# FFN gate and up computed by token for chunks 0 to 9, with the product turned by VectorE and sixteen SBUF transfers

## What is computed

```python
def swiglu(x, w_gate, w_up, w_down):
    return (jax.nn.silu(x @ w_gate) * (x @ w_up)) @ w_down
...
        y = swiglu(rms_norm(h, g[0]), ffn_w_gate[i, 0], ffn_w_up[i, 0], ffn_w_down[i, 0])
        h = h + 0.5 * rms_norm(y, g[1])
```

## Time and profile before

| | |
|---|---|
| median of 3 runs | 1010.06 us (1009.65 to 1010.57) |
| the profiled execution | 1009.73 us |
| its span, first to last instruction | 1007.9 us |
| TensorE busy | 998.5 us, 99% |
| VectorE, ScalarE, GpSimd busy | 638.5, 519.8, 116.7 us |
| granted TensorE clock | 1.000 |
| DMA, mean | 188 GB/s, 189.55 MB |

### The profile page before, as it was taken

One profiled execution on the slowest core, in us unless ns is written; L12 is line 12 of the kernel. 1 busy time (PEld: TensorE's weight loads), 2 busy tenths in 40 slices (PEclk: granted clock), 3 DMA queues, 4 the chain that ended last, 5 costly groups with the idle time before them and its releaser, 6 DMA issues. The chain is left out here.

```text
span 1007.9 us, 13834 instructions
## 1 busy us (share of the span) xinstructions
PE 998.5 (99%) x5701; PEld 850.5 (84%) x5701; DVE 638.5 (63%) x768; ACT 519.8 (52%) x709; POOL 116.7 (12%) x214
## 2 busy tenths in 40 slices
PE   8999999999999999999999999999999999999997
PEld 7888888898777888888889888888888789888886
DVE  5666565757796765556576555557568776565654
ACT  5544445644674564444464544445457555444452
POOL 1000000222373200000030000001103320000000
PEclk9999999999999999999999999999999999999999
DMA  9767778367404465557735555592485346565551
GB/s 272 250 204 250 235 254 295 114 188 221 157 2 126 134 216 194 193 183 239 264 100 191 187 190 194 182 331 87 146 280 165 136 132 195 181 207 173 204 178 73
DMA packets 138422, 189.55 MB, mean 188 GB/s; under 512 B 7442, under 2 KB 120439, under 8 KB 138360
## 3 DMA queue, kind: packets, MB, share of 16 engines
q1 hardware_dynamic: 133734, 172.83, 52.3%
q0 software_dynamic: 4480, 15.77, 4.7%
q10 hardware_dynamic: 146, 0.07, 0.0%
HBM read 185.99 MB, written 1.09 MB: 186 GB/s over the span
## 5 line engine op out<-in xcount | busy, mean ns | idle before, releaser
L815 DVE TENSOR_TENSOR wlo<-raw,whi 128x2048 fp32r<-128x2048 f32 x140 | 321.2, 2294 | 121.2 <-ACT whi L554 121.2
L1239 PE MATMUL ps<-xhl,whi 128*128 128x512 f32 (+1 forms) x1664 | 370.5, 374 | 0.0
L1239 PEld LDWEIGHTS ps<-xhl,whi 128*128 128x128 f32 x1664 | 293.1, 188 | 55.2 <-issue 2.4
L554 ACT ACTIVATE whi<-raw 128x2048 fp32r<-128x2048 f32 x145 | 276.9, 1910 | 28.9 <-DMA raw<-in_fox_w_in 9.0
L1239 PEld LDWEIGHTS ps<-xhl,wlo 128*128 128x128 f32 x1536 | 196.1, 191 | 6.9 <-issue 0.4
L1239 PE MATMUL ps<-xhl,wlo 128*128 128x256 f32 x1536 | 199.8, 283 | 0.0
L1239 PE MATMUL ps<-whi,hhi 128*128 128x512 f32 x320 | 124.9, 390 | 0.0
L1239 PE MATMUL ps<-wlo,hhi 128*128 128x512 f32 x320 | 124.9, 390 | 0.0
L1239 PE MATMUL ps<-whi,hlo 128*128 128x512 f32 x320 | 124.5, 389 | 0.0
L1239 PE MATMUL ps<-whi,xhl 128*128 128x512 f32 (+1 forms) x464 | 114.1, 373 | 0.3 <-ACT xhl L594 0.3
L1239 PEld LDWEIGHTS ps<-whi,xhl 128*128 128x128 f32 x464 | 81.1, 190 | 15.8 <-issue 1.9
(11 more groups left out here) (176 smaller groups left out, 803.4 us busy)
## 6 DMA issues: line engine op xcount, KB each, us to landing
raw<-in_ffn_w_down SPq DMA_DIRECT2D x44, 1024.0 KB, 4.9
raw<-in_ffn_w_up SPq DMA_DIRECT2D x40, 1024.0 KB, 5.2
raw<-in_ffn_w_gate SPq DMA_DIRECT2D x37, 1024.0 KB, 5.1
raw<-in_fox_w_in SPq DMA_DIRECT2D x9, 1024.0 KB, 5.3
raw<-in_nsa_w_in SPq DMA_DIRECT2D x7, 1024.0 KB, 5.7
big<-in_nsa_cmp_w POOLq DMA_DIRECT2D x8, 512.0 KB, 6.9
raw<-in_nsa_w_out SPq DMA_DIRECT2D x4, 1024.0 KB, 5.6
raw<-in_fox_w_out SPq DMA_DIRECT2D x4, 1024.0 KB, 4.9
```

Source lines behind the costliest of these rows:

```text
L554: nc.scalar.activation(whi[:, u % RING, :], raw_of(u), ACT.Copy).then_inc(w_hi, 1)
L815: nc.vector.tensor_tensor(wlo[:, u % RING, :], raw_of(u), whi[:, u % RING, :].bitcast(F32), ALU.subtract).then_inc(w_lo, 1)
L1239: return nc.tensor.matmul(out_, l, r, start=start, stop=stop)
```

## The change

Chunks 1 to 9 are computed by token, as chunk 0 is: the input is stationary and gate and up weights move side by side, 512 columns. Their two units per chunk now hold the upper and the lower half of the model width, each with gate and up columns (`is_half`, `load_half`), so that such a unit is two DMAs of 512 KB. In the openings of FFNs 1 to 3 units 2 and 3 stay columns of gate and up, and the FFN takes the opening that FoX has. Chunk 10 stays by feature. The product of chunks 0 to 9 has tokens on the partitions. One VectorE operation transposes it in blocks of 32 x 32 into `turned` (the space of `up_sb`), and SP issues 16 transfers inside SBUF, 32 partitions x 128 values each, that bring the blocks to their places in `prod_sb`. ScalarE and VectorE then take the high and the low part in two operations each, which reorder the blocks along the row. The copies and additions L602, L606, L888, L897 remain for chunk 10 alone, and `product_T` is gone. PSUM banks GB and OB alternate by chunk (`chunk_bank`).

SP's order around it: load of unit u+5, the 16 transfers of chunk c, load of unit u+6, where u is the first unit of chunk c. The diff, cut to its core:

```diff
+                if not is_half(u):
+                    sp.dma_start(raw_of(u).rearrange("p (a n) -> p a n", a=a), src).then_inc(arrival_of(u), 16)
+                    return
+                halves = raw_of(u).rearrange("p (k j n) -> p k j n", k=KT // 2, j=2)
+                sp.dma_start(halves[:, :, 0, :], src[0]).then_inc(arrival_of(u), 16)
+                sp.dma_start(halves[:, :, 1, :], src[1]).then_inc(arrival_of(u), 16)
+
+            def load_half(u, w_g, w_u, c, h):
+                load(u, None, [w[h * D // 2:(h + 1) * D // 2, c * UC:(c + 1) * UC].rearrange("(k p) n -> p k n", p=P) for w in (w_g, w_u)])
...
+            def swap_blocks(f, c):
+
+                sp.wait_ge(turned_ready, (NCH - 1) * f + c + 1)
+                for q in range(4):
+                    for i in range(4):
+                        sp.dma_start(prod_sb[32 * q:32 * q + 32, P * i:P * i + P], turned[32 * i:32 * i + 32, P * q:P * q + P]).then_inc(swapped_in[f], 16)
...
+                    if kind == "ffn" and (j in (5, 7) or j >= 9 and j % 3 == 0 and j < 31):
+                        swap_blocks(FFN_OF[s], {5: 0, 7: 1}.get(j, j // 3 - 1))
...
             def silu(f, u0, c):
-                if c == 0:
-                    act.wait_ge(unit_done, u0 + 1)
-                    if f > 0:
-                        act.wait_ge(prod_ready, NCH * f)
-                    src = first_unit(f, 0)
+                if c == NCH - 1:
+                    act.wait_ge(gate_sum, f + 1)
+                    src = silu_sb.rearrange("p (a n) -> p a n", a=2)
                 else:
-                    act.wait_ge(gate_sum, (NCH - 1) * f + c)
-                    src = silu_sb.rearrange("p (a n) -> p a n", a=2)
+                    act.wait_ge(unit_done, u0 + 1 if f == 0 and c == 0 else columns_done(u0, c))
+                    if c or f:
+                        act.wait_ge(prod_ready, NCH * f + c)
+                    src = by_tokens(f, c, 0)
                 nc.scalar.activation(silu_sb.rearrange("p (a n) -> p a n", a=2), src, ACT.Silu).then_inc(silu_ready, 1)
 
             def hidden_hi(f, u0, c):
-                if c == 0:
-                    act.wait_ge(prodT_mm, f + 1)
-                    src = ps[:, PTB, :]
-                else:
+                if c == NCH - 1:
                     act.wait_ge(prod_ready, NCH * f + c + 1)
-                    src = prod_sb
-                if 2 <= c < NCH - 1:
+                    nc.scalar.activation(xhi[:, 0:2, :], prod_sb.rearrange("p (a n) -> p a n", a=2), ACT.Copy).then_inc(hhi_ready, 1)
+                    return
+                act.wait_ge(swapped_in[f], 256 * (c + 1))
+                if c >= 2:
                     act.wait_ge(unit_done, down_unit(u0, c - 2) + 1)
-                dst = xhi[:, 0:2, :] if c == NCH - 1 else hhi[:, c % 2, :, :]
-                nc.scalar.activation(dst, src.rearrange("p (a n) -> p a n", a=2), ACT.Copy).then_inc(hhi_ready, 1)
+                src = prod_sb.rearrange("p (i t k n) -> p k t i n", i=4, t=TT, k=2)
+                dst = hhi[:, c % 2, :, :].rearrange("p k (t i n) -> p k t i n", t=TT, i=4)
+                for k in range(2):
+                    last = nc.scalar.activation(dst[:, k], src[:, k], ACT.Copy)
+                last.then_inc(hhi_ready, 1)
...
+                for c in range(1, NCH - 1):
+                    u = gate_unit(u0, c) if c > 1 else u0 + 1
+                    silu(f, u0, c)
+                    if c > 1:
+                        hi(u + 4)
+                    hi(u + 5)
+                    if s == 0 and c == 1:
+                        act.wait_ge(gw_in, 16 * 3)
+                        nc.scalar.activation(ghi[:, :, :], gw, ACT.Copy).then_inc(ghi_ready, 1)
+                    hidden_hi(f, u0, c)
+                    if c < NCH - 2:
+                        hi(u + 6)
...
+            def turn_product(f, c):
+
+                dve.wait_ge(prod_ready, NCH * f + c + 1)
+                src = prod_sb.rearrange("p (a q n) -> p a q n", a=4, q=4)
+                dst = turned.rearrange("p (q a n) -> p a q n", q=4, a=4)
+                nc.vector.transpose(out=dst, in_=src).then_inc(turned_ready, 1)
...
+                src = prod_sb.rearrange("p (i t k n) -> p k t i n", i=4, t=TT, k=2)
+                hi_, lo_ = (v[:, c % 2, :, :].rearrange("p k (t i n) -> p k t i n", t=TT, i=4) for v in (hhi, hlo))
+                for k in range(2):
+                    last = nc.vector.tensor_tensor(lo_[:, k], src[:, k], hi_[:, k].bitcast(F32), ALU.subtract)
+                last.then_inc(hlo_ready, 1)
...
+                for c in range(1, NCH - 1):
+                    u = gate_unit(u0, c) if c > 1 else u0 + 1
+                    if c == 1 and s == 0:
+                        lo(u + 4)
+                    product(f, u0, c)
+                    if c == 1:
+                        turn_product(f, c)
+                        if s:
+                            lo(u + 4)
+                        lo(u + 5)
+                        if s == 0:
+                            dve.wait_ge(pre_mm, 1)
+                            nc.vector.tensor_copy(smallT[:, :], ps[:, YB + 1, 0:36])
+                            nc.vector.tensor_copy(vec[:, :], ps[0:H, YB + 1, 64:64 + SCORES]).then_inc(pre_evac, 1)
+                    else:
+                        turn_product(f, c)
+                        lo(u + 4)
+                        lo(u + 5)
+                    hidden_lo(f, c)
+                    if c < NCH - 2:
+                        lo(u + 6)
...
+            def half_rows(u, h, bank):
+
+
+                w_h, w_l = (w[:, u % RING, :].rearrange("p (k n) -> p k n", k=KT // 2) for w in (whi, wlo))
+                pe.wait_ge(w_hi, u + 1)
+                for t in range(TT):
+                    for k in range(KT // 2):
+                        for v in (xhi, xlo):
+                            mm(ps[:, bank + t, :], v[:, KT // 2 * h + k, t * P:(t + 1) * P], w_h[:, k, :], h == 0 and k == 0 and v is xhi, False)
+                pe.wait_ge(w_lo, u + 1)
+                for t in range(TT):
+                    for k in range(KT // 2):
+                        last = mm(ps[:, bank + t, :], xhi[:, KT // 2 * h + k, t * P:(t + 1) * P], w_l[:, k, :], False, h == 1 and k == KT // 2 - 1)
+                last.then_inc(unit_done, 1)
...
-                if KINDS[s] == "fox":
+                if KINDS[s] != "nsa":
...
+                open_sublayer(s)
                 if s == 0:
-                    open_sublayer(s)
-                    twin_features(u0 + 2, OB, product_T)
-                else:
-                    open_sublayer(s, product_T)
-                if s == 0:
-                    twin_features(u0 + 3, GB)
+                    for h in range(2):
+                        half_rows(u0 + 2 + h, h, chunk_bank(1))
                     setup()
...
+                for c in range(2, NCH - 1):
+                    pe.wait_ge(prod_ready, NCH * f + c - 1)
+                    for h in range(2):
+                        half_rows(gate_unit(u0, c) + h, h, chunk_bank(c))
+                    if s == 0 and c == 2:
+                        pe.wait_ge(pre_evac, 1)
+                    pe.wait_ge(hlo_ready, NCH * f + c - 1)
+                    u = down_unit(u0, c - 2)
+                    rows(u, u % RING, left_of(c - 2), c == 2)
+                for j in range(2):
+                    pe.wait_ge(prod_ready, NCH * f + NCH - 2 + j)
+                    twin_features(gate_unit(u0, NCH - 1) + j, chunk_bank(NCH - 1 + j))
```

More of the change, by code:

```diff
@@ L69, with is_half @@
     EARLY[U0[n] + 4] = 4
+def is_half(u):
+    s = max(n for n in range(NSUB) if U0[n] <= u)
+    j = u - U0[s]
+    return KINDS[s] == "ffn" and (2 if s == 0 else 4) <= j < 28 and (j < 6 or j % 3 != 0)
 def arrivals(u):
     if u in EARLY:
-        return 16 * sum(EARLY[v] == EARLY[u] for v in EARLY if v <= u)
-    return 16 * sum(v % RING == u % RING and v not in EARLY for v in range(u + 1))
+        return 16 * sum((2 if is_half(v) else 1) for v in EARLY if EARLY[v] == EARLY[u] and v <= u)
+    return 16 * sum((2 if is_half(v) else 1) for v in range(u + 1) if v % RING == u % RING and v not in EARLY)
 C_ID, C_MASK, C_VALID, C_A1, C_A2, C_R, C_NEG, C_SEL = 0, 128, 384, 386, 402, 418, 420, 436
@@ L142, in trunk @@
         up_sb = work[:, 1024:1536]
+        turned = work[:, 1024:1536]
         squares = work[:, 0:1024]
@@ L214, in trunk @@
         YB, GB, UB, OB, MB = 0, 4, 5, 6, 7
-        PTB, NGB = YB + 2, YB + 2
+        NGB = YB + 2
         HB = MB
@@ L238, in trunk @@
         silu_ready, prod_ready, hhi_ready, hlo_ready = sem("silu_ready"), sem("prod_ready"), sem("hhi_ready"), sem("hlo_ready")
-        prodT_mm = sem("prodT_mm")
+        turned_ready = sem("turned_ready")
+        swapped_in = [sem(f"swapped{f}_in") for f in range(4)]
         ghi_ready, glo_ready = sem("ghi_ready"), sem("glo_ready")
@@ L281, in down_unit, with chunk_bank, by_tokens, columns_done @@
             return u0 + 6 + 3 * c - (c > 8) * 2 * (c - 8)
```

(49 more changed lines are left out.)

74 lines of the change are left out of this document (26 added, 48 removed).

## The result

The changed kernel takes 1235.05 us, the median of four runs (1231.64 to 1236.61), against 1009.86 for the kernel before in the same session. The ratio is 1.2222, 95% interval 1.2203 to 1.2242. The forecast of 1005 has the wrong sign, and its range ends 208 us too low. The profiled execution has a span of 1229.8 us.

A forecast was written before the change was run, and what follows sets the result against it. TensorE, busy 998.5 of 1007.9 us, was taken as the bound: 1009.7 - 8.8 (matmuls, transposes) + 0.3 (FFNs 1 to 3) + 3.5 (first FFN) = 1004.7 profiled, so 1005.0 as median; range 1001 to 1027.

The forecast's parts named there:

- TensorE's matmuls, 8.8 us: TensorE's stream: wide matmuls by token and dropped transposes save 5.9, 2.5 and 0.4 us, together 8.8; a chunk takes 16.39.
- The transpose, 0.69: VectorE's block transpose of the product: taken at 0.69 us from a copy's row, 1.22 if it needs two passes.
- The sixteen transfers, 16 x 0.35 = 5.6 us, at most 6.6: SP's queue, each chunk: sixteen issues at 0.35 us each hold SP for 5.6 us, between 5.1 and 6.6.
- rival (b): The closed chain over SP, ScalarE and VectorE becomes the bound; at 0.40 per issue 14 us slower, 1024; chance 0.32.
- The load, 5.19: Weight load on SP behind the transfers: 5.19 us until ScalarE's `hi` starts, the same taken for two 512 KB halves.
- Landing, 1.9: The last of a chunk's transfers lands 1.9 us after its issue, as a 64 KB load does.
- Rival (c): Small transfers do not overlap their fixed part: 30 us until the last lands, some 1650 us in all; chance 0.02.
- The new loop: Closed chain of load, `hi`, `lo`, product, transpose and transfers, without TensorE: 16.46 us against TensorE's period of 16.39.
- The start of the chain, room of 0.6, and 24 turns: FFN openings: 0.6 us to spare covers six turns each 0.07 long; FFNs 1 to 3 lose 0.3; 24 turns in four FFNs.
- The first FFN loses 3.5, its neighbours nothing: First FFN: late units, turns without room and POOL's loads cost 3.5 us, between 1 and 8; FFNs 1 to 3 next to nothing.
- What would show it: Signs in the profile after: chunks of 16.4 us, waits for `whi` at first half units; steady chunks over 16.8 if the chain bounds.
- a second sign: TensorE's waits naming `hlo` or `wlo` of down units would mean the transfers' landing is late, not their issue.

The follow-up runs named there:

- the probe: The kernel before with extra unused DMAs issued by SP behind six loads of the last FFN, in groups differing by shape and source: 1009.6 us (one run).

## Why the prediction was wrong, point by point

- *TensorE's matmuls, 8.8 us.* Right, and a little more: 10.5 without the transfers. A chunk is 16.32 and not 16.39: 48 wide matmuls take 581.24 - 570.36 = 10.88 instead of 10.92, and the down unit 5.44 instead of 5.47; 33 chunks of 0.25 are 8.2 instead of 5.9.
- *The transpose, 0.69.* It takes 0.711, little more than the copy's 0.677 that it was taken from the earlier trace rows. The rule of one element per cycle and lane (the Trainium skill, "Vector Engine (DVE) Microarchitecture Reference", 3.8) agrees with that.
- *The sixteen transfers, 16 x 0.35 = 5.6 us, at most 6.6.* This is the step that failed: they take 10.05. All of the earlier trace rows have HBM as their source, and the probe shows that such issues in a row cost 0.46 and those out of SBUF 0.63. (Why the row of exactly this shape out of HBM held SP for 0.31 at the start and sixteen of them 0.46 each is open.) The trace of before had closer rows, which I did not use: SP's stores out of SBUF at the end, and GpSimd's transfers out of SBUF. From the timeline of the kernel before:

```profile
218.66 0.64 POOL L503 DMA_DIRECT2D pairs<-work  x1 [12.86 <-DVE work L1128]
219.29 0.60 POOL L504 DMA_DIRECT2D pairs<-work  x1
...
1004.80 1.00 SPq L419 DMA_DIRECT2D out<-res  x2
```

  0.50 to 0.64 us each. At 0.5 the chain would have been 16.46 + 16 x 0.15 = 18.9 us, well over TensorE's period, and rival (b) the forecast.
- *The load, 5.19.* It took 6.56 in the turn above and 5.86 with eight transfers. The rows were of one 1 MB load, issued alone. Here two halves are issued behind a burst: 0.62 until the second issue, which then held SP for 1.50 or 0.51.
- *Landing, 1.9.* Right for most: from 1.7 us, with a median of 1.8 (the longest 6.2), and hidden behind the load except where the load goes first. Rival (c), no overlap of small transfers and 1650 us, is refuted by the turn above: sixteen have landed within 740.54 - 727.72 = 12.8 us, not 30. The Trainium skill ("DMA: Bandwidth & Descriptors", Bandwidth) warns of transfers under 64 KB. The direction that it points in was right. What cost was not the bytes of the transfers, though: with a sixteenth of the bytes the time is the same, and one row costs SP as much as 32.
- *The new loop.* Right in every link and their order; measured to 22.21 with no remainder. Rival (b), which carried the mechanism at a chance of 0.32, was sized with 0.40 per issue and got 1024.
- *The start of the chain, room of 0.6, and 24 turns.* Wrong by the same term. With 4.45 us more per turn there is no room anywhere: the 36 turns of four FFNs, the openings' too, lose 213.6 / 36 = 5.9 each. In FFN 2 the first two turns take 15.1 and 17.5 us against 8.2 and 11.8 without transfers.
- *The first FFN loses 3.5, its neighbours nothing.* It does start worse, by 58.8 - 51.6 = 7 us against the others' mean, beside the 51.6 that the chain takes from each.
- *What would show it.* The signature was right: waits for `whi` at the first half unit and steady chunks over 16.8 us, for rival (b). But a second sign came as well, waits for `wlo` of down units (26 of the 38.8 us, behind chunk 9), and what the prediction would have read from it, a late landing, is wrong: there too it is a load behind the sixteen issues.

The range failed for a reason of its own. Its bound for an issue, 0.41, was the longest of a few rows of one kind, so it bounded nothing for the other kind. The chain came out within 0.1 us of the period, and that alone should have made the range wide: each 0.1 us on an issue is 1.6 us per turn, near 60 us over 36 turns.

## What to carry to other kernels

Count DMA issues as instructions of the engine that issues them, and price them from rows with the same source, the same queue and as many in a row; sixteen small ones out of SBUF are 10 us, whatever they carry. Before a burst is put into a queue, ask what is queued behind it and whether that leads back to the burst: such a loop costs its whole excess in every turn. If it does, split the burst over queues that have nothing urgent behind it; here that, with the changes of order on ScalarE and VectorE, turned 22% slower into 0.4% faster.

## What the runs showed of the hardware that I had not expected

- An issue on SP costs 0.63 us out of SBUF, 0.46 out of HBM in a row, 0.37 alone. On GpSimd's queue the SBUF transfers hold the engine for 3.93 / 8 = 0.49.
- After the wait of 2.73 us in the turn above TensorE's next 16 wide matmuls take longer: until the next group 751.70 - 746.38 = 5.32 us instead of 736.23 - 732.60 = 3.63. A table of three such stretches shows the clock (stretch: us, TensorE's busy time, granted clock, DMA share, GB/s):

```profile
732.60:736.23 3.63, 3.63 (x17) 1.00 0.11 27
746.38:751.70 5.32, 5.32 (x16) 0.68 0.52 199
753.52:757.14 3.62, 3.62 (x17) 1.00 0.12 27
```

  The granted clock is 0.68 over the 5.32 us behind the wait, between half (1.2 GHz) for a part of it and full (2.4 GHz) for the rest, and full again in the next group. So this wait of 2.7 us costs 4.4 of TensorE's time. Such stretches fit that TensorE is busy for 1068.6 us here and for 988.1 without transfers. In the turns the chain sets the period and hides it; where TensorE is the bound it would be paid.
- Reads of 64 KB out of HBM, four in a row beside the stream of weights, land in 4.9 us (median), against 1.9 for the one in the earlier trace rows. Which of the differences between the two is the cause was not tested.
